# First gate's rows into the arena, router weights out of the tables' buffer

## The reference, cut to what matters

```python
shift1, scale1, gate1, shift2, scale2, gate2 = modulation(cond, w_mod, b_mod)   # (1024) @ (1024 x 6144)
h = x * (1 + scale1) + shift1
na_q, ..., ret_q, ret_k, ret_v, ret_g, diff_q, ... = project(h, w_in)
...                                        # neighbourhood attention, retention, differential attention
ret_o = head_layer_norm(ret_o) * ret_gn_w + ret_gn_b
y = concat(na_o, ret_o * silu(ret_g), diff_o) @ w_out
x = layer_norm(ALPHA * x + gate1 * y, ln1_w, ln1_b)
h = x * (1 + scale2) + shift2
g = softmax(h @ router_group)              # 4 groups; the top group, in it the top 2 of 8 experts
e = h @ router_expert
y = sum of the chosen experts: (silu(h @ w_gate) * (h @ w_up) * weight) @ w_down   # 32 experts, FF = 256
x = layer_norm(ALPHA * x + gate2 * y, ln2_w, ln2_b)
```

## Time and profile before

| | |
|---|---|
| median of 3 runs | 1177.9 us (1176.45 to 1179.03) |
| profiled execution: time / span | 1180.55 us / 1178.6 us |
| TensorE busy | 1086.1 us (92%) |
| VectorE / ScalarE / GpSimd busy | 429.7 / 211.5 / 178.8 us |
| loads issued by SP (q1) | 313.47 MB, 69.9% of 16 engines' span |
| mean granted TensorE clock | 0.959 |

### The profile page before, as it was taken

One profiled execution on the slowest core, in us unless ns is written; L12 is line 12 of the kernel. 1 busy time (PEld: TensorE's weight loads), 2 busy tenths in 40 slices (PEclk: granted clock), 3 DMA queues, 4 the chain that ended last, 5 costly groups with the idle time before them and its releaser, 6 DMA issues.

```text
span 1178.6 us, 16670 instructions
## 1 busy us (share of the span) xinstructions
PE 1086.1 (92%) x6670; PEld 714.3 (61%) x6671; DVE 429.7 (36%) x1029; ACT 211.5 (18%) x530; POOL 178.8 (15%) x180
## 2 busy tenths in 40 slices
PE   5899999989999999978989999999898999999784
PEld 1766878558756555545448567775687655555531
DVE  0034545266743111121162345442587312122116
ACT  0322324200111111110112233421002111111100
POOL 0442010041111111110113000201411111111001
PEclk8899999999989999998999999999998999999997
DMA  8999222497799999999999222237859999999981
GB/s 355 255 259 364 79 72 86 158 332 285 251 423 417 419 418 418 419 417 410 353 295 316 75 72 76 89 135 255 305 206 362 372 392 419 418 418 418 420 337 59
DMA packets 102624, 342.77 MB, mean 291 GB/s; under 512 B 20300, under 2 KB 61308, under 8 KB 70420
## 3 DMA queue, kind: packets, MB, share of 16 engines
q1 hardware_dynamic: 88400, 313.47, 69.9%
q0 software_dynamic: 12416, 18.79, 5.0%
q10 hardware_dynamic: 1732, 9.45, 2.0%
HBM read 337.76 MB, written 28.25 MB: 311 GB/s over the span
## 4 chain that ended last, share of the span: by engine, by line
PE 74%; DMA 9%; SPq 5%; issue 4%; DVE 3%; POOL 2%; ACT 2%; POOLq 0%; ACTq 0%; DVEq 0%
PE ps L1020 16%; PE ps L1317 16%; PE ps L1013 8%; PE ps L1197 8%; PE ps L1341 7%; SPq L875 5%; DMA arena<-in_exp_w_down 3%; PE ps L1281 3%; DMA ring<-in_exp_w_up 3%; DMA ring<-in_w_in 2%; PE ps L1274 1%; PE ps L1113 1%; PE ps L960 1%; PE ps L1381 1%; PE ps L1159 1%
## 5 line engine op out<-in xcount | busy, mean ns | idle before, releaser
L1317 PE MATMUL ps<-ring,arena 128*64 128x256 f32 x1376 | 199.2, 402 | 10.7 <-DMA ring<-in_exp_w_up 7.0
L1020 PE MATMUL ps<-ring,arena 128*128 128x256 f32 (+1 forms) x960 | 200.1, 367 | 6.2 <-DMA ring<-in_w_in 3.6
L1020 PEld LDWEIGHTS ps<-ring,arena 128*128 128x128 f32 x960 | 170.2, 194 | 29.0 <-issue 5.2
L1317 PEld LDWEIGHTS ps<-ring,arena 128*64 128x64 f32 x1376 | 119.8, 144 | 63.5 <-issue 21.9
L1013 PE MATMUL ps<-arena,ring 128*128 128x384 f32 x288 | 96.9, 490 | 0.7 <-ACT arena L1604 0.5
L2174 DVE TENSOR_TENSOR arena<-arena,ps 128x256 f32<-128x256 f32 x32 | 13.5, 422 | 226.5 <-PE ps L1317 150.9
L1197 PE MATMUL ps<-ring,arena 128*128 128x256 f32 x384 | 89.6, 397 | 0.0
L1341 PE MATMUL ps<-ring,arena 128*64 128x512 f32 x304 | 82.0, 611 | 4.7 <-DMA ring<-in_exp_w_down 3.2
L1197 PEld LDWEIGHTS ps<-ring,arena 128*128 128x128 f32 x384 | 76.7, 201 | 11.2
L1013 PEld LDWEIGHTS ps<-arena,ring 128*128 128x128 f32 x288 | 53.3, 190 | 36.8 <-issue 1.8
L2400 POOL DMA_INDIRECT arena<-token_rows,arena x30 | 30.6, 1019 | 272.1 <-PE ps L1281 141.7
(11 more groups left out here) (294 smaller groups left out, 1409.1 us busy)
## 6 DMA issues: line engine op xcount, KB each, us to landing
ring<-in_exp_w_up SPq DMA_DIRECT2D x48, 1024.0 KB, 22.7
ring<-in_w_mod SPq DMA_DIRECT2D x45, 1024.0 KB, 5.2
ring<-in_exp_w_gate SPq DMA_DIRECT2D x40, 1024.0 KB, 19.4
ring<-in_exp_w_down SPq DMA_DIRECT2D x39, 1024.0 KB, 26.1
ring<-in_w_in SPq DMA_DIRECT2D x24, 1024.0 KB, 14.3
arena<-in_exp_w_down SPq DMA_DIRECT2D x14, 1024.0 KB, 25.1
arena<-in_exp_w_gate SPq DMA_DIRECT2D x12, 1024.0 KB, 23.9
ring<-in_w_out SPq DMA_DIRECT2D x8, 1024.0 KB, 12.9
```

The lines of the kernel that those rows point to most:

```text
L1020: mm = pe.matmul(out[:, 0:w], hT[:, ch, where * P:(where + 1) * P], unit(l, name)[:, ch, 0:w], start=(ch == 0), stop=(ch == CH - 1))
L1317: mm = pe.matmul(ps[64 * w:64 * w + 64, 2 * (i % 2) + kind, 0:FF], xgT[i % 2][:, ch, w * SLOTS:(w + 1) * SLOTS], weights[:, ch * FF:(ch + ...
```

## The change

gate1 gets no place any more: its two row tiles lie in the arena at columns 0 to 2047, where the retention has its work tiles (`scb`, `rt`, `snew`, `sq_r`); so their load waits until the outputs and the statistics of all three retention tiles are done. `bias` and `tables` become one buffer, of which place 16 is the first 2048 columns and place 17 the next 2048. `rw` gets a buffer of its own and `norm_s` moves into the tables; place 17 is then free when the third retention tile is normalised (`ret_normed`), as place 15 is. The release lists are changed to match.

```diff
--- before.py
+++ after.py
@@ -111,12 +111,14 @@
 
 C_NAO, C_RETO, C_DIFFO = C_DK, C_RK, C_DQ
 MIXT = 3072
+GATE1 = 0
 Z = 6144
 H2, H2T, XR, XGT = 10240, 7168, 7168, 9216
 PLACE_12, PLACE_13, PLACE_14 = 3072, 5120, 11264
 SMALL = 2 * NA_W + 2 * DIFF_W + 6 * HD + RET_W
 GSEL, HIDDEN = 1536, 0
-TABLES = RET_HEADS * P + RET_W + DIFF_W + CH * (GROUPS + EXPERTS) + 6 * DIFF_D + 6 * 21 + 8 * RET_HEADS
+TABLES = RET_HEADS * P + RET_W + DIFF_W + 6 * DIFF_D + 6 * 21 + 8 * RET_HEADS + 4 * TILES * RET_HEADS
+BIAS_W = NA_HEADS * 6 * GRID_W
 ROUTE, YB = 13312, 14768
 GW, PT_LAST = GSEL + 384, GSEL + 768
 
@@ -202,7 +204,7 @@
 
 
 ROWS_LATE = {1: ("gate1", "shift2"), 2: ("scale2", "gate2")}
-ROW_FILLS = ("gate1", "shift2", "ln1", "scale2")
+ROW_FILLS = ("shift2", "ln1", "scale2")
 
 
 def front_order():
@@ -344,10 +346,10 @@
     fronts = sorted(LAST_JOB, key=lambda u: LAST_JOB[u])
     attended = JOB_NO["pT", 9, 13]
     gone += [u for u in fronts if LAST_JOB[u] < attended] + [("arena", BIAS_PLACE)]
-    gone += [u for u in fronts if LAST_JOB[u] >= attended] + [("arena", SMALL_PLACE)]
+    gone += [u for u in fronts if LAST_JOB[u] >= attended] + [("arena", SMALL_PLACE), ("arena", CONST_PLACE)]
     then = early_units(l + 1)
-    gone += [("wout", u) for u in range(OUT_UNITS)] + [("rows", "gate1")] + then[:4]
-    gone += [("rows", n) for n in ("shift2", "scale2")] + [("arena", i) for i in (RING, RING + 1, CONST_PLACE)]
+    gone += [("wout", u) for u in range(OUT_UNITS)] + then[:4]
+    gone += [("rows", n) for n in ("shift2", "scale2")] + [("arena", i) for i in (RING, RING + 1)]
     gone += then[4:6] + [("arena", RING + 2)] + then[6:] + [("rows", "ln1")]
     return gone + EXPERT_RELEASES
 
@@ -460,10 +462,12 @@
             return small[:, edge[0] - n:edge[0]]
         na_kc, na_vc, df_kc, df_vc = part(NA_W), part(NA_W), part(DIFF_W), part(DIFF_W)
         s0 = part(6 * HD).rearrange("p (a b c) -> p a b c", a=2, b=3)
-        bias = sb("bias", [P, NA_HEADS, 6, GRID_W])
         gnw = part(RET_W)
         assert edge[0] == SMALL == UNIT
-        tables_ = sb("tables", [P, TABLES])
+        biastab = sb("tables", [P, BIAS_W + TABLES])
+        bias = biastab[:, 0:BIAS_W].rearrange("p (h r c) -> p h r c", h=NA_HEADS, r=6)
+        tables_ = biastab[:, BIAS_W:]
+        rw = sb("rw", [P, CH, GROUPS + EXPERTS])
         taken = [0]
 
         def table(*dims):
@@ -476,9 +480,10 @@
                 return v.rearrange("p (a b c) -> p a b c", a=dims[0], b=dims[1])
             return v
         decay, gnb, dnw = table(RET_HEADS, P), table(RET_W), table(DIFF_W)
-        rw, lamp, lamt = table(CH, GROUPS + EXPERTS), table(4, DIFF_D), table(2, DIFF_D)
+        lamp, lamt = table(4, DIFF_D), table(2, DIFF_D)
         stats, lg = table(N_ATT, 6), table(4, 2, RET_HEADS)
-        assert taken[0] == TABLES >= UNIT
+        norm_s = table(4, TILES * RET_HEADS)
+        assert taken[0] == TABLES and BIAS_W + TABLES >= 2 * UNIT
         dec = sb("dec", [P, 2, RET_HEADS])
         brow = sb("brow", [DEPTH * 6 * D // 256, 256])
         lamk = sb("lamk", [P, 2])
@@ -487,7 +492,6 @@
         cdec = sb("cdec", [P, 2, 3])
         lam = sb("lam", [P, 8])
         diff_s = sb("diff_s", [P, 3, TILES * DIFF_HEADS])
-        norm_s = sb("norm_s", [P, 4, TILES * RET_HEADS])
         ln_s = sb("ln_s", [P, TILES, 20])
 
         ocount = sb("ocount", [1, DEPTH + 1], I32)
@@ -527,6 +531,8 @@
         z = at(Z, D)
 
         def row_tile(l, name, k):
+            if name == "gate1":
+                return at(GATE1 + k * D, D)
             return places_of_unit[SPOT[l, ("rows", name)][0]][:, k * D:(k + 1) * D]
 
         def late_tile(l, name, k):
@@ -592,8 +598,8 @@
 
         ring_full = [signal(f"ring_full{s}") for s in range(PLACES)]
         places_of_unit = [ring[:, s, :] for s in range(RING)] + [at(PLACE_12, UNIT), at(PLACE_13, UNIT), at(PLACE_14, UNIT)]
-        places_of_unit += [small[:, 0:UNIT], bias[:, :, :, :].rearrange("p h r c -> p (h r c)")[:, 0:UNIT]]
-        places_of_unit.append(tables_[:, 0:UNIT])
+        places_of_unit += [small[:, 0:UNIT], biastab[:, 0:UNIT]]
+        places_of_unit.append(biastab[:, UNIT:2 * UNIT])
         const_in = signal("const_in")
         toeplitz_out = signal("toeplitz_out")
         x_in = [signal(f"x_in{i}") for i in range(2)]
@@ -732,12 +738,12 @@
             elif kind == "wout":
                 eng.wait_ge(y_ready.sem, y_ready.at(l, TILES))
             elif kind == "rows":
-                done = {"gate1": gated, "ln1": ln1_done}.get(what[0], h2_ready)
+                done = ln1_done if what[0] == "ln1" else h2_ready
                 eng.wait_ge(done.sem, done.at(l, TILES))
             elif kind == "arena":
                 if what[0] == BIAS_PLACE:
                     wait_alone(eng, negmax_ready, negmax_ready.at(l, N_ATT))
-                elif what[0] == SMALL_PLACE:
+                elif what[0] in (SMALL_PLACE, CONST_PLACE):
                     wait_alone(eng, ret_normed, ret_normed.at(l, TILES))
                 else:
                     wait_alone(eng, logits_ready, logits_ready.at(l, TILES))
@@ -780,8 +786,11 @@
 
             def load_rows(l, name):
 
-                before = SPOT[l, ("rows", name)][2]
-                wait_released(sp, *before)
+                if name == "gate1":
+                    sp.wait_ge(ret_ready.sem, ret_ready.at(l, TILES))
+                    wait_alone(sp, ret_var, ret_var.at(l, TILES))
+                else:
+                    wait_released(sp, *SPOT[l, ("rows", name)][2])
                 for k in range(2):
                     if name == "ln1":
                         src = (ln1_w, ln1_b)[k][l:l + 1]
```

## The result

The change makes the kernel slower. In its rounds it took 1186.4 us at the median (1185.27 to 1188.02) and the kernel before 1178.1 us (1176.45 to 1179.03): ratio 1.0068, 95% interval 1.0056 to 1.0080, or 8.3 us. The two intervals don't meet, so the size is known only as 8 to 12 us; the sign and the mechanism are the same in both. The forecast was 1178.3 us with a range of 1172.4 to 1183.8: both measurements lie outside. The profiled execution took 1188.02 us with a span of 1186.2, its mean granted TensorE clock is 0.954 (0.959 before).

The account below looks back on a forecast made before the run. Expert stages were taken to start bound by TensorE and end bound by the weight stream. -1.7 (layer 0) - 0.5 (tail) + 2.6 (layer 1) = +0.4 us on 1177.9 gave 1178.3 us, range 1172.4 to 1183.8.

Parts of the forecast that it names:

- Part 1, layer 0: Row loads before the router: gate1's wait delays scale2 by 8.0 us, minus 4.72 slack; TensorE stalls 3.3 us.
- The bounds below it: Smaller shifts of layer 0's scale2: 6.0 us with row tiles at full bandwidth, 1.5 were the store not behind rows.
- Part 1, layer 1: Same row loads in layer 1: shift 7.67 us, slack 5.04, so TensorE is 2.6 us late.
- The slack of 5.04: Layer 1's first h2 tile: ready at 864.27, wanted by TensorE at 869.31, a slack of 5.04 us.
- The rival: Slower side, chance 0.20: the stall doubles the 1.6 us clock loss at each layer's third output projection; total 1181.5 us.
- Part 2, layer 0: Two units loaded earlier are worth 5.0 us; with the later start, layer 0's expert stage ends 1.7 us sooner.
- The stream never runs dry: Layer 0 around the router: 21st unit issued at 340.9, before the stream ends at 344.7, so the 5.0 us holds.
- Part 3: Tail of layer 0: renumbered places change TensorE's wait for gathered rows by 0 to -1.9 us; -0.5 taken.
- both ways: Layer 0's experts: -1.7 us by the weight stream, -1.8 by TensorE giving back 5.1 us of weight waits.
- Part 2, layer 1: Stream runs dry at the router anyway, so two units earlier gain none; the 2.6 us lateness stays to the end.
- Part 4: New addresses of rw and norm_s: router products and statistics run the same instructions, 0.

Follow-up runs that it names:

- gate1 last: The change, with gate1's row load moved behind scale2 in both layers: 1172.1 us against 1178.7 for the kernel before, ratio 0.9957.
- the reordered one: The kernel before, with only gate1's load moved behind scale2 and no unit loaded earlier: 1177.7 us against 1178.1, ratio 1.0004.
- the kernels kept busy: The change with identity transposes filling TensorE's stall: in both layers 1181.3 us, repeated 1181.6; in layer 1 only 1185.6.
- its control: The changed kernel itself measured again, nothing altered: 1189.7 us against 1178.1 for the kernel before, ratio 1.0105.

## Why the prediction was wrong

**Part 1, layer 0: right.** The shift of scale2 against `out_proj(0, 0)` is 8.15 us (forecast 8.00), the first column grows by 3.5 us (forecast 3.3), 2.76 of them idle. The bounds below it (6.0 and 1.5 us) did not come about. The Trainium skill (DMA: Bandwidth & Descriptors, Queues, rings and completion order) says that descriptors of a ring are consumed in ring order; the 11.24 us agree. So do the kernels with gate1 last and the reordered one: with 2 MB of rows ahead of the store instead of 3, SP waits 4.80 and 4.33 us from the store to scale2 instead of 7.88.

**Part 1, layer 1: the size was off.** The first column grows by 5.1 us, not 2.6 (idle time: 5.39). The slack of 5.04 was right; the shift is 10.2 us instead of 7.67, since the stretch of eight DMAs grew from 11.01 to 13.63 us. The forecast had taken it over unchanged. These 2.6 us lie behind the store (10.17 against 7.28 us); why it came back later is not known.

**The term that failed most: the clock, set to nothing.** The sum held the stall alone and left the clock to a rival. Measured from tile 0 to tile 1 it is 3.2 us in layer 0 and 3.6 us in layer 1, and the kernels kept busy show that it goes when the stall is filled. The rival was the right mechanism at half its price: it doubled the 1.6 us of the third output projection, which came about as 1.5 and 1.1 us more, and did not count the transposes (1.97 instead of 1.05 us in layer 1) and the router products (3.63 instead of 2.11 in layer 0, 3.62 instead of 1.97 in layer 1). The row of the router's products was in the same time line, with 16 short instructions right behind the stall. The Trainium skill (TensorE: Matmul & The Clock Gate, The HAM clock gate) has an idle engine's gate fall to half rate; the 0.50 in the windows after the stall agrees. The rival had a chance of 0.20, and even its price would have left the sum short.

**Part 2, layer 0: the right kind, half to two thirds of the size.** "The stream never runs dry" was wrong. The third column falls by 3.2 us in the change (3.0 in its control, 3.6 in gate1 last; 2.2 to 3.6 in the other kernels with two units), not by 5.0, and 0.7 of the 3.2 are the tail (Part 3); with one unit it falls by 1.5 to 2.8. With two units already gone, SP has nothing to issue between 316.59 and 321.93, where the first of the next layer's early modulation units gives back its place; before, it still had two units to issue there, at 313.06, and the DMA share stays at 0.87 or above from 304 to 324. The windows of the change and of gate1 last:

```profile
320.00:324.00 4.00, 4.00 (x48) 1.15 (x40) 3.17 (x12) 0.00 (x0) 0.57 (x1) 1.00 0.44 74
```

```profile
312.00:316.00 4.00, 4.00 (x43) 2.28 (x46) 3.26 (x7) 0.00 (x0) 1.52 (x1) 1.00 0.63 233
316.00:320.00 4.00, 3.63 (x34) 1.69 (x26) 3.41 (x18) 0.78 (x2) 0.00 (x0) 1.00 0.79 233
```

The idle share is 0.56 x 4 = 2.2 us in the one and (0.37 + 0.21) x 4 = 2.3 us in the other, so the hole doesn't come from the stall; 5.0 less 2.2 is 2.8, near the 2.5 measured without the tail. The forecast counted places at scale2 and at the router, and not the early units' releases between. The second of the "both ways" failed as well: the waits of TensorE for weights between 480 and 530 did not shrink (5.5 us, 5.1 in the earlier trace rows), though the experts' first product comes 5.0 us later behind the first output projection. Stream and TensorE were late together.

**Part 2, layer 1: nearly right.** Forecast 0; the last column falls from 258.61 by 0.3 us in the change, 0.2 in its control and 0.95 to 1.3 us in the four kernels with units ahead whose rows are late in at most one layer; what sets these apart is not known. The whole loss ahead of the experts is passed on to the end, as forecast.

**Part 3 (-0.5): about right.** TensorE waits 1.2 us for the gathered rows in the change and 1.4 in its control, 1.9 before; the wait stands just ahead of the fourth cut, so it lies in the third column. The rest of the tail can't be told from the 242 to 245.5 us that the stretch between the layers takes in all twelve. **Part 4** (0): the router products at the second tile read `rw` from its new buffer in 1.98 us, as the kernel before does from the tables.

By these cuts layer 0 with its tail was forecast at -2.2 and layer 1 at +2.6, and they measured +3.5 and +8.4. Of the 11.5 us between, 6.7 are the clock, 2.5 the longer row stretch of layer 1, 2.3 the units of layer 0.

## What to carry to other kernels

In an in-order queue of loads, a load with a new condition belongs behind everything that has none: the freed buffer was worth -6.6 us with the wait placed last and +8 to +12 us with it placed first. A new idle stretch on TensorE ahead of short matmuls has two prices: count the gap, and then reprice every matmul behind it at the lower clock, up to where the windows show 1.00 again; here the second was 6.7 us and the first 8.7. And where slack is eaten up by a chain of transfers, take the chain's length with a margin, since its 11 us did not stay 11 us when it was moved.

## What the runs showed of the hardware that was not expected

- The stretch with the router products and the third output projection mostly takes one of a few lengths, and they differ in the granted clock: 17.48 us (1.00 throughout), 19.16 us (the usual one, the clock falling inside the projection), 22.1 to 22.8 us (clock at 0.50 from the stall on). The eleven stretches without a stall fall on the first two to within 0.02 us, and no edit explains which of them one gets. Stretches behind a filled or a like stall also took 17.78, 19.48 and 20.68 us.
- The row loads, each to 128 partitions, start slowly: 76, 221 and 160 GB/s in the first six microseconds in layer 1, and then, still rows, 358 and 426, as much as the units. The windows of the change:

```profile
839.00:841.00 2.00, 2.00 (x7) 1.64 (x6) 0.07 (x1) 0.67 (x2) 1.77 (x2) 0.50 0.33 76
841.00:843.00 2.00, 2.00 (x10) 1.76 (x10) 0.00 (x0) 0.00 (x0) 1.84 (x3) 0.99 0.75 221
843.00:845.00 2.00, 2.00 (x11) 1.75 (x10) 0.00 (x0) 0.00 (x0) 1.54 (x2) 1.00 0.70 160
845.00:847.00 2.00, 2.00 (x11) 1.76 (x10) 0.00 (x0) 0.00 (x0) 0.00 (x0) 1.00 0.97 358
847.00:849.00 2.00, 2.00 (x11) 1.77 (x10) 0.00 (x0) 0.00 (x0) 0.00 (x0) 1.00 1.04 426
```

- One and the same kernel measured 1.0068 and 1.0105 of the kernel before on two occasions, with intervals that don't touch. An interval from one set of rounds doesn't hold what differs between sets, and what that was stays open. It weakens every comparison here between kernels of different sets by 3 to 4 us, above all the price of the clock by the medians.
